# Opening of a hybrid pooling / state-space / MoE layer: another order of the first loads, and dummy products between the modulation's products

## The reference, cut to what matters

```python
mod = jax.nn.silu(c) @ prm['w_ada'] + prm['b_ada']            # w_ada: 1024 x 6144
sh1, sc1, g1, sh2, sc2, g2 = jnp.split(mod, N_MOD, axis=-1)
h = modulate(rmsnorm(x, prm['norm1_g']), sh1, sc1)            # h * (1 + scale) + shift
u = h @ prm['w_in']                                           # 1024 x 1024
pool_out, new_buf = pool_mixer(u[..., :POOL_WIDTH], ...)
ssm_out, nh_re, nh_im = ssm_mixer(u[..., POOL_WIDTH:], ..., ssm_b_re, ssm_b_im, ssm_c_re, ssm_c_im, ...)
mix = jnp.concatenate([pool_out, ssm_out], axis=-1) @ prm['w_out']
x = x + g1[:, None, :] * mix
x = x + g2[:, None, :] * hier_moe(modulate(rmsnorm(x, prm['norm2_g']), sh2, sc2), ...)
```

## Time and profile before

| | us |
|---|---|
| median of 3 runs | 1182.48 (1181.56 to 1183.22) |
| the profiled execution's own time | 1183.54 |
| its span, first to last instruction | 1181.7 |
| TensorE busy | 1085.3 (92%) |
| DVE busy | 776.4 (66%) |
| ACT busy | 508.1 (43%) |
| POOL busy | 283.1 (24%) |
| mean rate of the DMA engines | 208 GB/s |

### The profile page before, as it was taken

One profiled execution on the slowest core, in us unless ns is written; L12 is line 12 of the kernel. 1 busy time (PEld: TensorE's weight loads), 2 busy tenths in 40 slices (PEclk: granted clock), 3 DMA queues, 4 the chain that ended last, 5 costly groups with the idle time before them and its releaser, 6 DMA issues. The chain is left out here.

```text
span 1181.7 us, 18292 instructions
## 1 busy us (share of the span) xinstructions
PE 1085.3 (92%) x5541; PEld 804.8 (68%) x5542; DVE 776.4 (66%) x1276; ACT 508.1 (43%) x715; POOL 283.1 (24%) x347
## 2 busy tenths in 40 slices
PE   3799999999958899999999899999999999999991
PEld 2357777676546567787788556777877877778750
DVE  5556575747889973468887787655666555555384
ACT  5233242421132325446665243544555444455372
POOL 0046262616041000030000002333333333333212
PEclk9799999999988999999999999999999999999996
DMA  9834655557686449386765458887899777775597
GB/s 282 306 107 118 190 141 178 154 149 220 194 219 135 156 147 256 151 234 214 249 219 214 161 214 271 230 271 213 218 285 262 219 213 220 211 200 106 106 374 307
DMA packets 168381, 245.71 MB, mean 208 GB/s; under 512 B 65912, under 2 KB 124056, under 8 KB 165455
## 3 DMA queue, kind: packets, MB, share of 16 engines
q1 hardware_dynamic: 141697, 177.35, 47.0%
q0 software_dynamic: 14384, 49.53, 17.2%
q10 hardware_dynamic: 12246, 18.14, 4.6%
HBM read 169.36 MB, written 75.84 MB: 207 GB/s over the span
## 5 line engine op out<-in xcount | busy, mean ns | idle before, releaser
L126 PE MATMUL experts_psGU<-weights_we_hi,experts_x_hi 128*128 (+1 forms) x344 | 143.2, 416 | 2.9 <-issue 1.7
L128 PE MATMUL experts_psGU<-weights_we_lo,experts_x_hi 128*128 (+1 forms) x344 | 136.0, 395 | 0.0
L127 PE MATMUL experts_psGU<-weights_we_hi,experts_x_lo 128*128 (+1 forms) x344 | 135.8, 395 | 0.0
L126 PE MATMUL front_psM<-front_hT_hi,front_w_hi 128*128 128x512 f32 x256 | 106.5, 416 | 0.9 <-DVE front_hT_lo L1008 0.9
L127 PE MATMUL front_psM<-front_hT_hi,front_w_lo 128*128 128x512 f32 x256 | 101.2, 395 | 0.0
L128 PE MATMUL front_psM<-front_hT_lo,front_w_hi 128*128 128x512 f32 x256 | 101.1, 395 | 0.0
L2503 POOL DMA_INDIRECT acc_d<-experts_o_sb,experts_to_col x40 | 69.3, 1733 | 130.0 <-issue 73.1
L126 PEld LDWEIGHTS experts_psGU<-weights_we_hi,experts_x_hi 128*128 128x128 f32 x344 | 64.6, 188 | 28.8 <-issue 15.7
L2677 DVE TENSOR_TENSOR experts_x_lo<-experts_psX,experts_x_hi 128x1024 fp32r<-128x1024 f32 x42 | 51.4, 1224 | 37.5 <-ACT experts_x_hi L2567 37.5
L2667 DVE TENSOR_TENSOR weights_we_lo<-weights_we_raw,weights_we_hi (+1 forms) x64 | 75.4, 1219 | 0.0
L128 PEld LDWEIGHTS experts_psGU<-weights_we_lo,experts_x_hi 128*128 128x128 f32 x344 | 64.6, 188 | 15.5
(11 more groups left out here) (521 smaller groups left out, 2522.7 us busy)
## 6 DMA issues: line engine op xcount, KB each, us to landing
front_raw<-in_w_ada SPq DMA_DIRECT2D x32, 512.0 KB, 4.0
weights_we_raw<-in_exp_w_gate SPq DMA_DIRECT2D x16, 1024.0 KB, 5.9
weights_we_raw<-in_exp_w_up SPq DMA_DIRECT2D x16, 1024.0 KB, 12.5
weights_wd_raw<-in_exp_w_down SPq DMA_DIRECT2D x16, 1024.0 KB, 13.2
front_xraw<-in_x_prompt SPq DMA_DIRECT2D x4, 2048.0 KB, 9.9
front_raw<-in_w_ada SPq DMA_DIRECT2D x8, 1024.0 KB, 14.7
part_d<-middle_ev ACTq DMA_DIRECT2D x16, 512.0 KB, 3.6
middle_xt<-in_x_prompt SPq DMA_DIRECT2D x16, 512.0 KB, 4.8
```

Of the source, the lines that this page charges most:

```text
L126: pe.matmul(out, l_hi, r_hi, start=start, stop=False)
L127: pe.matmul(out, l_lo, r_hi, start=False, stop=False)
L128: return pe.matmul(out, l_hi, r_lo, start=False, stop=stop)
```

## The change

Two things. In SP's list the transfers of C and B go behind `w_load(0)` and the first tokens (the two helper functions that stood between are written ahead of them). In TensorE's list dummy products (`keep_busy`, into the second half of `psM`, which nobody uses yet) are put in: four ahead of the first modulation product, two behind each of the first seven, one behind the eighth, and two behind the transposes of the modulation: 21 in all.

```diff
--- before.py
+++ after.py
@@ -312,23 +312,22 @@
                     sp.dma_start(arow[:, i, :], a[n][0].rearrange("(k g) p -> k (g p)", g=2)).then_inc(s["tab_in"], 16)
                 sp.dma_start(dtrow[:, 0:2], a["ssm_log_dt"][0].rearrange("(k g) -> k g", g=2)).then_inc(s["tab_in"], 16)
 
+                def ada_first(t):
+                    if t >= 4:
+                        sp.wait_ge(s["ada_mm"], t - 3)
+                    sp.dma_start(raw1[t % 4][:], ada[t, :, 0:2 * D]).then_inc(raw1_in[t % 4], 16)
+
+                def w_load(h):
+                    sp.dma_start(wraw[h][:], w[:, :, h * BLK:(h + 1) * BLK]).then_inc(w_in[h], 16)
+
+                w_load(0)
+                sp.dma_start(xraw[:], a["x_prompt"][0, 0:BLK, :].rearrange("(j p) d -> p j d", p=P)
+                             ).then_inc(s["x_in"], 16)
                 for i, n in enumerate(("ssm_c_re", "ssm_c_im")):
                     sp.dma_start(crow[:, i, :].rearrange("h (g p) -> h g p", g=G),
                                  a[n][0].rearrange("g h p -> h g p")).then_inc(s["c3_in"], 16)
                 for i, n in enumerate(("ssm_b_re", "ssm_b_im")):
                     sp.dma_start(brow[:, i, :], a[n][0].rearrange("(k g) p h -> k (g p h)", g=2)).then_inc(s["b3_in"], 16)
-
-                def ada_first(t):
-                    if t >= 4:
-                        sp.wait_ge(s["ada_mm"], t - 3)
-                    sp.dma_start(raw1[t % 4][:], ada[t, :, 0:2 * D]).then_inc(raw1_in[t % 4], 16)
-
-                def w_load(h):
-                    sp.dma_start(wraw[h][:], w[:, :, h * BLK:(h + 1) * BLK]).then_inc(w_in[h], 16)
-
-                w_load(0)
-                sp.dma_start(xraw[:], a["x_prompt"][0, 0:BLK, :].rearrange("(j p) d -> p j d", p=P)
-                             ).then_inc(s["x_in"], 16)
                 sp.dma_start(x_smp[:], x_s).then_inc(s["xs_in"], 16)
                 for t in range(4):
                     ada_first(t)
@@ -665,8 +664,10 @@
                                           idt[0:PAIRS, 0:PAIRS])
                 mm.then_inc(s["x_fill"], 1)
                 pe.wait_ge(s["ct_sb"], 1)
+                keep_busy(pe, psM[:, 1, :], idt[:], 4)
                 for t in range(NA - 1):
                     ada_first(t)
+                    keep_busy(pe, psM[:, 1, :], idt[:], 2)
                 def v_bank(pe, n):
                     if n == 2:
                         pe.wait_ge(s["u_evac"], KD * NBLK)
@@ -682,10 +683,12 @@
                     mm = pe.transpose(psX[:, 1, t * TS:(t + 1) * TS], x_smp[:, t * P:(t + 1) * P], idt[0:TS, 0:TS])
                 mm.then_inc(s["xs_turn"], 1)
                 ada_first(NA - 1)
+                keep_busy(pe, psM[:, 1, :], idt[:], 1)
                 pe.wait_ge(s["mod_sb"], 1)
                 for q in range(4):
                     mm = pe.transpose(psC[:, q * P:(q + 1) * P], modA[:, q * P:(q + 1) * P], idt[:])
                 mm.then_inc(s["modt_ps"], 1)
+                keep_busy(pe, psM[:, 1, :], idt[:], 2)
                 for b in range(NBLK):
                     for m in range(KD):
                         product(b, m)
```

More of the change, by code:

```diff
@@ L313, in _ @@
                 sp.dma_start(dtrow[:, 0:2], a["ssm_log_dt"][0].rearrange("(k g) -> k g", g=2)).then_inc(s["tab_in"], 16)
-                for i, n in enumerate(("ssm_c_re", "ssm_c_im")):
-                    sp.dma_start(crow[:, i, :].rearrange("h (g p) -> h g p", g=G),
-                                 a[n][0].rearrange("g h p -> h g p")).then_inc(s["c3_in"], 16)
-                for i, n in enumerate(("ssm_b_re", "ssm_b_im")):
-                    sp.dma_start(brow[:, i, :], a[n][0].rearrange("(k g) p h -> k (g p h)", g=2)).then_inc(s["b3_in"], 16)
                 def ada_first(t):
@@ L331, in _ @@
                              ).then_inc(s["x_in"], 16)
+                for i, n in enumerate(("ssm_c_re", "ssm_c_im")):
+                    sp.dma_start(crow[:, i, :].rearrange("h (g p) -> h g p", g=G),
+                                 a[n][0].rearrange("g h p -> h g p")).then_inc(s["c3_in"], 16)
+                for i, n in enumerate(("ssm_b_re", "ssm_b_im")):
+                    sp.dma_start(brow[:, i, :], a[n][0].rearrange("(k g) p h -> k (g p h)", g=2)).then_inc(s["b3_in"], 16)
                 sp.dma_start(x_smp[:], x_s).then_inc(s["xs_in"], 16)
```

## The result

The changed kernel takes 1191.59 us (median of 3 runs, 1189.15 to 1192.27) against 1182.48: a ratio of 1.0069, 95% interval 1.0055 to 1.0082, some 8 us more. It was measured twice more beside the experiments, with more runs: 1.0053 (1.0039 to 1.0068) and 1.0066 (1.0051 to 1.008). The mean of the three is about 7.4 us. The direction was as forecast; 1187.5 was 4.1 us too low, and 1191.59 lies 1.3 us above the range. The profiled execution took 1191.59 us, its span is 1189.8 where it was 1181.7.

A forecast was written before the change was run, and what follows sets the result against it. TensorE bounds the kernel: start 26.4, plus 23.7 of dummies, blocks and transposes, plus 2.3 at half clock, puts the eighth block at 52.4 against 47.36. So 1182.48 + 5.0 = 1187.5 us; range 1183.6 to 1190.3.

The forecast's parts named there:

- C's transposes: TensorE ahead of the first block: start at 19 to 20 us instead of 8.62, with B's ended near 26.
- The last three dummies: Behind the eighth product (one) and the result's transposes (two): they lie in existing waits and cost nothing.
- DVE's last preparatory operation: In the opening: moves from 37.01 to about 48 us, with room since the addition waiting for it comes later too.
- The order alone: Moved loads without dummies: TensorE half a microsecond late on the first block, absorbed by pauses between blocks; no cost.
- moves everything behind it by the same amount: Behind the opening: TensorE is the bound, so what the opening gains or loses shifts all later work equally.
- The step: One of the first seven blocks on TensorE: product 0.95 plus two dummies of 0.86, 2.67 us, against blocks 2.5 apart.
- The start: TensorE done with B's transposes at 26.4 us, with weights and tokens ending near 15 and C landing at 19.6.
- my two bounds: End of B's transposes on TensorE: 26.7 us with C landed at 19.6, or 23.9 with C at 16.6.
- The head: Four dummies ahead of the first block, starting at 1.2 GHz: half-clock loss 1.7 to 3.4 us, taken as 2.3.
- the dummies pay: Rival, opening: dummies only fill pauses at 2.4 GHz, eighth product at 45.3, 2.1 us earlier, 1180.4 us; 4%.
- break-even: Opening: for the dummies to cost nothing, TensorE would need to be done with B at 21.4 us.
- a second chain: Rival: C and B later, half clock through four dummies, one more fall: 8.6, 1191.1; or block 7's buffer late; 10%.

The follow-up runs named there:

- the fitted dummies: Against the kernel before, C and B first: 8 dummies ahead of the first block, then as many as each pause holds, 2 before the sample tokens' split wait; ratio 0.9987.
- the version with the norm's row late: Against the kernel before: dummies fitted to the pauses, C and B first, and the transfer of the norm's 1024 gains moved behind the eighth block; ratio 0.9991.

## Why the prediction was right in its mechanism and wrong in its size

**Right.** TensorE is the bound, and its own list is what became late: no wait for a block between the first and the eighth, granted clock 1.00 from 33 to 53 us, eighth product late and the first L126 with it (5.19 us behind it, as before). C's transposes were forecast for 19 to 20 us and B's end near 26; they came at 20.63 and 27.66. The last three dummies hide, as forecast: the same 5.19. DVE's last preparatory operation starts at 48.28 us, forecast about 48. The order alone costs next to nothing, as forecast: 0.44 us at the eighth product. That the whole shift is carried to the end holds in this execution, 7.6 us at the eighth product and 8.1 in the span, but not as closely as the prediction had it ("moves everything behind it by the same amount"): the other two executions of the change have 9.0 and 8.35 at the eighth product and 8.7 and 6.6 in the span, and the one with one dummy 1.5 and 5.5.

**Wrong: three terms of the sum.** The forecast had 26.4 + 5.74 (four dummies with the surcharge of the half clock) + 18.69 (seven steps of 2.67) + 1.55 (transposes) = 52.4. Measured: 27.66 + 5.43 + 20.28 + 1.61 = 54.98.

- *The step, +1.59 us.* This is the largest. "Behind a product of about 0.95 us ... two dummies of 0.86 make a step of 2.67 us" took the dense price for both dummies and 0.95 for the product. Measured: 1.00 for the product, 1.05 for the first dummy, 0.86 for the second, 2.91. So 0.05 of the 0.24 us are the product and 0.19 the first dummy. A row for it stood there: three products in a short run took 2.84, 0.95 each, and I used the value of a long run, 0.86. Each block has two changes of the stationary operand, condition to identity and back, and the time above the dense one (2.91 less 3 x 0.86, 0.33 us) appears in every step. The Trainium skill ("TensorE: Matmul & The Clock Gate", section "LDWEIGHTS (loading the stationary operand)") gives columns over 1.2 as the time of such a load in ns; an estimate by it is 107 for 128 columns and 27 for 32. This trace differs, and it decides: its loads last 0.19 us for the identity's 128 columns and 0.11 for the condition's 32. That the loads make up the excess fits, but no run here separates them from other causes.
- *The start, +1.26 us.* The tokens landed at 16.9, forecast 15. I took 395 GB/s from 4.0 us on, but that is the mean of a stretch already in flow, and the slice from 3.0 to 4.5 us moved 51. Behind them C landed 3.7 us after the tokens, at 20.6 (forecast 19.6), and TensorE's 7.0 us of transposes from there end at 27.66: beyond the later of my two bounds, 26.7, which did not allow for later tokens.
- *The head, -0.31 us* in the profile of the result, but +1.0 and +0.8 in the two other profiled executions (6.69 and 6.55 from the first dummy to the block). The bound I gave for it, 3.4 us of surcharge, holds; the value differs from one execution to the next.

Together 2.6 us of the 4.1 by which the median was missed. The other 1.5 is what the median of the first three runs lies above the opening's shift, 9.1 against 7.6, and the other two series do not show it: their medians are 7.3 and 7.1 above the kernel before. Against them the forecast was 2.1 to 2.3 us too low. That is near the 2.6, but not the same sum: in their profiled executions the eighth product is 4.0 and 3.4 us later than forecast, since the head is longer, and 1.7 us come back because the fall of clock behind the opening is missing.

**The range** ended at 1190.3 because it added the upper bound of the start at half clock (1.1 us) and a fall of clock (1.7), but no bound at all for the step, which had seven repetitions, and none for a later landing of the tokens. An error of 0.24 us a step was the largest term of the miss.

**The rivals.** That the dummies pay was rightly put low for this change: TensorE was done with B at 27.66, and break-even lay at 21.4. But the profile of the fitted dummies shows the effect itself: eighth product 0.2 us behind its landing. The rival called a second chain, at 1191.1 and 10%, was nearest to the median, and part of what it named did happen: C and B landed later (20.6 and 23.6 instead of 19.6 and 21.7), and in the other two executions the four first dummies passed almost wholly at half clock. Its buffers did not: no block was waited for. And it did not have the step. The chain that did come up is another, DVE's tables, and it ends last only once the dummies are fitted, by 0.13 us.

## What to carry to other kernels

Fillers that are to keep an engine's clock up cost nothing only inside a pause that the trace shows: count each with its switch of operand (1.06 here for a lone one, 0.86 for the next), and leave some of the pause (the fitted version left 0.35 to 0.64 us of each). Placed too early they miss their purpose: four that ended 4.77 us ahead of the block left it at half clock. An edit that makes an engine start late and one that fills its pauses must not be priced one by one: 0.4 and 3.0 us at one place became 7.6. And where a step is repeated seven times, its price deserves a bound of its own in the range.

## What the runs showed of the hardware that was not expected

- The transposes of C and B, 16x16, did not bring the clock up. In the version with none ahead, the first block ran for 1.93 us, the time of 1.2 GHz, right behind 7.0 us of such transposes back to back. The Trainium skill says of transposes that they don't count as busy for the clock in the same way ("TensorE: Matmul & The Clock Gate", section "Part 4: PE-mode transpose"); this row agrees, but it does not hold for all transposes of this case: in the kernel before the granted clock rose at 47.0 us, behind 1.9 us of a product and 2.4 us of 128x128 and 64x64 transposes, and the eighth product behind them took 1.07. Whether it is the size that makes the difference no run separates.
- The rise of the clock is not at a fixed distance from the work. The four dummies of the changed kernel took 5.50, 6.77 and 6.62 us in three executions, though they began at 27.66, 27.77 and 27.28 with the same work ahead and behind; with one dummy behind each block, the same four took 5.87.
- A granted full clock can be lost in a short pause: in the version with the dummies alone it was down 2.1 us behind their end (21.8 to 23.9), and with eight instead of four, which end 0.64 us ahead of the first block, that block takes 1.06. Nor is this a fixed distance: in the version with the norm's row late a pause of 1.68 us ahead of the first block left the clock full (1.06 us for the block).
- The issue of a transfer can itself last: in the changed kernel the second half of C took 3.19 us on SP's queue and the first half of B 5.09, against 0.49 and 0.48 before. So B's second half was not issued until 12.81 us. These stretches begin once some 4 MB have been asked for; in the kernel before, with C and B ahead, it is the sample tokens' issue (1.18 us) and the four blocks' (5.08) that last. It cost nothing here, as the tokens ahead landed only at 16.9, but what stands behind such an issue in SP's list waits with it.
- C and B pass slowly wherever they stand: the rate in the 1.5 us slices in which they pass behind the weights is 82 to 180 GB/s, against some 400 in the slices around them; it was 118 when they came first. From ACT's queue, beside the start of the weights, all queues moved 114 GB/s (1.8 to 8.4 us). Neither place nor queue made these 0.5 MB cheap.
